# Start addresses of the on-chip tiles in a fused three-layer kernel: 32 and 64 bytes past a multiple of 128, or at the multiple

## What is computed

```python
h = rms_norm(x)              # layer 1: one projection, w_in is 2048 x 7832
nsa  = attention(h)          #   8 heads: compressed, selected and window branches, gated
rwkv = recurrence(h, h_prev) #   RWKV-7, 16 heads of 64, a 64 x 64 state each
x = x + (gated nsa, rwkv) @ w_out
x = x + mla(rms_norm(x))     # layer 2: 16 heads, latent queries and keys of 512
x = x + diff_attn(rms_norm(x))   # layer 3: 8 heads, softmax(q1 k1) - lam * softmax(q2 k2)
```

## Time and profile before

| | |
|---|---|
| median of three executions | 3158.12 us |
| the three | 3154.66, 3158.12, 3159.01 us |
| the profiled execution | span 3154.7 us, 51,865 instructions |
| TensorE busy | 3118.6 us, 99% |
| VectorE, ScalarE, GpSimd busy | 1762.0, 1274.4, 193.0 us |
| bytes read from and written to HBM | 276.05 and 44.85 MB |
| DMA queue of the loads | 34.9% of the 16 engines' span |

### The profile page before, as it was taken

One profiled execution on the slowest core, in us unless ns is written; L12 is line 12 of the kernel. 1 busy time (PEld: TensorE's weight loads), 2 busy tenths in 40 slices (PEclk: granted clock), 3 DMA queues, 4 the chain that ended last, 5 costly groups with the idle time before them and its releaser, 6 DMA issues. The chain is left out here.

```text
span 3154.7 us, 51865 instructions
## 1 busy us (share of the span) xinstructions
PE 3118.6 (99%) x21457; PEld 2553.3 (81%) x21457; DVE 1762.0 (56%) x3081; ACT 1274.4 (40%) x2328; POOL 193.0 (6%) x154
## 2 busy tenths in 40 slices
PE   8999999999999999999999999999999999999999
PEld 6877777777878778788888888888888888888787
DVE  4335565565666744644457776335556655665822
ACT  4124333433444422523346665323344434443421
POOL 0000000001011101000001010110000000000000
PEclk9999999999999999999999999999999999999999
DMA  8433333332232353343332213534223323332452
GB/s 253 114 81 91 90 94 96 100 111 60 70 98 70 110 165 108 109 110 100 107 104 54 61 51 121 163 104 117 87 81 94 94 76 99 94 95 81 158 163 77
DMA packets 494639, 324.25 MB, mean 103 GB/s; under 512 B 27194, under 2 KB 449693, under 8 KB 494406
## 3 DMA queue, kind: packets, MB, share of 16 engines
q1 hardware_dynamic: 494374, 320.94, 34.9%
q10 hardware_dynamic: 32, 0.01, 0.0%
HBM read 276.05 MB, written 44.85 MB: 102 GB/s over the span
## 5 line engine op out<-in xcount | busy, mean ns | idle before, releaser
L538 DVE TENSOR_TENSOR WLT<-AR,WHT 128x1024 fp32r<-128x1024 f32 (+1 forms) x430 | 527.0, 1231 | 668.1 <-ACT WHT L532 667.7
L550 PE MATMUL PS<-XH,WHT 128*128 128x512 f32 (+1 forms) x2224 | 896.0, 403 | 3.7 <-issue 1.4
L552 PE MATMUL PS<-XH,WLT 128*128 128x512 f32 (+1 forms) x2224 | 872.0, 392 | 0.0
L532 ACT ACTIVATE WHT<-AR 128x1024 fp32r<-128x1024 f32 (+1 forms) x430 | 447.5, 1043 | 604.9 <-PE PS L552 475.0
L551 PE MATMUL PS<-XL,WHT 128*128 128x512 f32 (+1 forms) x1712 | 668.7, 391 | 0.0
L550 PEld LDWEIGHTS PS<-XH,WHT 128*128 128x128 f32 (+1 forms) x2224 | 416.7, 187 | 101.6 <-issue 9.5
L552 PEld LDWEIGHTS PS<-XH,WLT 128*128 128x128 f32 (+1 forms) x2224 | 416.9, 187 | 97.2
L551 PE MATMUL PS<-ARR,WHT 128*128 128x512 f32 x1024 | 404.6, 395 | 0.0
L551 PEld LDWEIGHTS PS<-XL,WHT 128*128 128x128 f32 (+1 forms) x1712 | 320.9, 187 | 71.0 <-issue 4.0
L551 PEld LDWEIGHTS PS<-ARR,WHT 128*128 128x128 f32 x1024 | 192.4, 188 | 40.3 <-issue 0.2
L550 PE MATMUL PS<-XL,WHT 128*128 128x512 f32 x512 | 203.3, 397 | 0.1
(11 more groups left out here) (511 smaller groups left out, 5197.8 us busy)
## 6 DMA issues: line engine op xcount, KB each, us to landing
AR<-b_w_in SPq DMA_DIRECT2D x128, 512.0 KB, 4.0
AR<-w_in SPq DMA_DIRECT2D x122, 512.0 KB, 4.0
AR<-a_w_in SPq DMA_DIRECT2D x48, 512.0 KB, 4.5
AR<-w_out SPq DMA_DIRECT2D x32, 512.0 KB, 4.2
AR<-a_w_out SPq DMA_DIRECT2D x32, 512.0 KB, 4.0
AR<-b_w_out SPq DMA_DIRECT2D x32, 512.0 KB, 4.1
proj_scratch<-AR SPq DMA_DIRECT2D x33, 256.0 KB, 2.1
residual_scratch<-RES SPq DMA_DIRECT2D x8, 1024.0 KB, 5.4
```

What stands on the lines that cost most here:

```text
L532: self.nc.scalar.activation(self.shaped(self.high, n), self.shaped(self.raw, n), ACT.Copy).then_inc(self.s_high, 1)
L538: self.nc.vector.tensor_tensor(self.shaped(self.low, n), self.shaped(self.raw, n), f32(self.shaped(self.high, n)), ALU.subtract).then_inc( ...
L550: mm(out, wh, xh[k0 + c], start=(start and c == 0), stop=False)
L552: last = mm(out, wl, xh[k0 + c], start=False, stop=(stop and c == nk - 1))
```

## The change

Every large tile, and ARR with it, is put at a multiple of 128 bytes. A new method, fill_line, allocates an unused tile that fills up to the next such multiple; it is called ahead of RES (PAD_HEAD) and behind the constants (PAD_C). ARENA, the size of AR in words, grows from 17,064 to 17,088, a multiple of 32 words, so that what lies behind AR is at a multiple too. In the mixer of layer 1 the three input rows take 1,568 words in place of 1,539; the tiles with odd sizes (WC2, OMK) are taken last, and in nsa W2 is taken ahead of KCT.

By these sizes the addresses after are: RES, XH, XL and C as before; PAD_C 107,680 (96 bytes), PRM 107,776, STG 108,800, AR 112,896, EXT 181,248, ONESR 195,584, WHT 196,096, WLT 212,480, end 228,864. From PRM on all have remainder 0. RES before starts at 1,152, which is 9 x 128. In the mixer of layer 1, W2, TOK and BON go from remainder 12 to 0, and TW, GTI, HB, ST, LW and RQ from 76 to 0; in nsa W2 from 12 to 0. No scratch tile of layer 1 changes its region.

```diff
--- before.py
+++ after.py
@@ -57,7 +57,8 @@
 BQ0, BK0, BV0, BG0 = 0, 16, 32, 48
 LAM_INIT = 0.8 - 0.6 * float(np.exp(-0.3))
 NPROJ = 62
-ARENA = 17064
+ARENA = 17088
+LINE = 128
 SCRATCH = 1024
 EXTRA = 7
 
@@ -158,7 +159,9 @@
 
 def aligned(nc):
 
-    return (nc.sbuf_base + 31) // 32 * 32
+    base = (nc.sbuf_base + 31) // 32 * 32
+    assert base % LINE == 0, base
+    return base
 
 
 class Kernel:
@@ -167,6 +170,7 @@
     def __init__(self, nc, ctx, dram):
         self.nc, self.ctx, self.d = nc, ctx, dram
         cc, nconst = const_cols()
+        self.fill_line("PAD_HEAD")
         at = [aligned(nc)]
         self.RES = self.sb("RES", [P, KT, T])
         at.append(aligned(nc))
@@ -180,6 +184,7 @@
         self.XHT, self.XLT = ([x[:, c, :] for c in range(KT)] for x in (self.XH, self.XL))
         at.append(aligned(nc))
         self.C = self.sb("C", [P, nconst])
+        self.fill_line("PAD_C")
         self.CR = nc.alloc_sbuf_tensor_at("CR", [P, 3, T], F32R, offset=at[3] + 4 * cc["bones"][0])
         self.PRM = self.sb("PRM", [P, 2 * P])
         at.append(aligned(nc))
@@ -219,6 +224,12 @@
 
         x = self.AR[:, 24 * T:30 * T].rearrange("p (n t) -> p n t", t=T)
         return x[:, 0:TB, :], x[:, TB, :], x[:, TB + 1, :]
+
+    def fill_line(self, name):
+
+        gap = -((self.nc.sbuf_base + 31) // 32 * 32) % LINE
+        if gap:
+            self.sb(name, [P, gap // 4])
 
     def sb(self, name, shape, dt=F32):
         return self.ctx.enter_context(self.nc.sbuf_tensor(name, shape, dt))
@@ -652,8 +663,13 @@
 def first_pair_inputs(k):
 
     flat = k.RES[:, :, :].rearrange("p a t -> p (a t)")
-    n = 3 * (T + 1)
-    return flat[:, 0:n], flat[:, n:n + P], flat[:, n + P:n + P + T + 1]
+    n, m = 3 * (T + 1), lines(3 * (T + 1))
+    return flat[:, 0:n], flat[:, m:m + P], flat[:, m + P:m + P + T + 1]
+
+
+def lines(n):
+
+    return (n + LINE // 4 - 1) // (LINE // 4) * (LINE // 4)
 
 
 def nsa(k, st, tiles, ntile, res_out):
@@ -676,11 +692,12 @@
     HL, Q = KV[0][:, 0:2, :], KV[1][:, 0:2, :]
     Z, EV, S = room.tiles(2), room.tiles(2), room.tiles(3)
     PTC, TM = room.take(T), room.take(T)
-    VC, KCT = room.take(NKV * HD), room.take(NKV * NCMP)
+    VC = room.take(NKV * HD)
+    W2 = room.tiles(2, P)
+    KCT = room.take(NKV * NCMP)
     G = room.take(TB * NGATE).rearrange("p (b n) -> p b n", n=NGATE)
     MX, SIGM, HB, CST = room.take(24), room.take(NKV * NCMP), room.take(NKV * NCMP), room.take(1)
     TAB = room.take(NH)[0:NBUCKET + 1, :]
-    W2 = room.tiles(2, P)
     OH = E.rearrange("p h m -> p (h m)")[0:NBUCKET + 1, 0:T + P]
     WIN = S
     NG = NKV * NCMP
@@ -1205,12 +1222,11 @@
 
     flat, W2, WA = first_pair_inputs(k)
     take(2 * T)
-    take(3 * (T + 1))
+    take(lines(3 * (T + 1)))
     take(P)
     AR = k.STG
     TOK = chunks(5)
     BON2 = [take(T) for _ in range(2)]
-    WC2 = [take(NCH) for _ in range(2)]
     TW = take(T)
     GTI, HB, ST = (take(T).rearrange("p (c f) -> p c f", f=CH) for _ in range(3))
     IN = flat.rearrange("p (n t) -> p n t", t=T + 1)
@@ -1227,9 +1243,10 @@
     P1TA = take(2 * T).rearrange("p (c j f) -> p c j f", j=2, f=CH)
     LOT = [x.rearrange("p (c f) -> p c f", f=CH) for x in (take(T), take(T))]
     RQ = take(4 * 2 * TB).rearrange("p (n b e) -> p n b e", n=4, e=2)
-    OMK = take(NPAIR)
     QT, Y = take(T), take(T)
     EV = room.tiles(2)
+    OMK = take(NPAIR)
+    WC2 = [take(NCH) for _ in range(2)]
     FACTOR, SG = layer1_factor(k), k.EXT[:, 1, :]
     NL = len(LEVELS)
     C, B = k.c, k.PSB
```

## The result

The changed kernel takes 3164.11 us (median of seven executions, 3162.03 to 3165.41), the kernel before 3155.29 (seven, 3153.21 to 3159.01). The ratio is 1.0028, with a 95% interval of 1.0018 to 1.0037: it is slower by 0.28%, or 9 us, where 12 us less were forecast. The time lies 3 us above the upper end of the stated range (3161).

A forecast was written before the change was run, and what follows sets the result against it. TensorE, busy for 99% of the span, was taken as the bound, through the pace of its matmuls. The terms, 6.8 + 5.1 = 11.9 us less, against the median of 3158.1 gave 3146 us, with a range from 3124 to 3161.

The forecast's parts named there:

- Term 3: WHT and WLT, read by every triple, go from 64 to 0: taken as nothing, ends one step a triple either way.
- Term 1: Layer 3's 1,024 triples with ARR as moving tile: from 693.3 to 686.7 ns each, 6.8 us less.
- Term 2: Layer 3's 512 token triples with ARR as stationary tile: from 353.2 to 343.3 ns each, 5.1 us less.
- Terms 4 to 6: fp32 matmuls, DVE and ACT, and DMA into AR: each taken as nothing; fp32 and DMA with ends 1 us either way.
- The slower one: Weights and moving rows at the same place slow 1,712 triples, now at 686.7 ns, by one step: 3164 us; chance 0.10.
- The larger gain: With weights and rows both at 0, 2,736 triples drop one step, to 680 ns: 3128 us; chance 0.10.
- 0.72 for faster: The whole kernel: the chance given to its being faster by over 0.2%.

The follow-up runs named there:

- e1_weights: The kernel before with one filler of 192 bytes ahead of the weights, so only WHT and WLT move; 3164.65 us, ratio 1.0032.
- e5_rows_only: The changed kernel without its edits to nsa, rwkv and first_pair_inputs, and with a 64-byte filler ahead of the weights; 3145.46 us, ratio 0.9973.
- the first sweep: A separate kernel of matmul triples alone, 136 sets of addresses; with the weights stepped by 16 bytes, 680.0 to 702.8 ns a triple.
- e2_all_equal: The changed kernel with a 128-byte filler behind the constants, every large tile at remainder 128 modulo 256; 3133.55 us, ratio 0.9931.
- e8_all_zero: e2_all_equal with a 128-byte filler behind PAD_HEAD, so all large tiles lie at multiples of 256; 3132.82 us, ratio 0.9936.
- the second sweep: A second kernel of matmuls alone: pairs, triples, token form and fp32 by distance; pairs of 512 columns took 226.7 ns at 0, 233.3 at 128.
- e4_after_weights128: The changed kernel with a filler of 128 bytes ahead of the weights, so only WHT and WLT move; 3146.79 us, ratio 0.9973.

## Why the prediction was wrong

**What bounds the kernel: right.** The pace of the matmuls set the time and nothing else did. The difference of 8.4 us is in the distances from start to start. That the pace hangs on addresses was right as well.

**Term 3 is the step that failed.** "WHT and WLT from 64 to 0, which every triple reads: taken as nothing." It cost 10.4 ns on each triple of layers 1 and 2, more than the one step that the term gave as its end, and 17.8 us in all, more than terms 1 and 2 were to bring; e1_weights shows it alone. Its evidence was misread. The rows name the moving tile first, and by the kernel's code the moving side of L3621 to L3623 is XH and EXTR and the stationary side XL and CR, the other way round than the part on who uses which tile has it (in L3660 and L3661 likewise the stationary side is ONESR). XH, XL and CR lie a multiple of 256 bytes apart, distance 0; L3622, with XL by EXTR, is at distance 64. These rows were taken as a sample of "weights at 0"; two in three of them were a sample of "both at the same place", which the change did not bring about. The same goes for the scores, both sides in RES. The remainder was counted modulo 128, as the change itself counts, and no view was asked whether 0 and 128 modulo 256 are the same. The rows already held tiles at distance 0, 192 and 160; sorted by distance instead of by place, they would have asked for a row at distance 128 before anything was taken as nothing. Among the rows shown there was none, and the kernel before was unlikely to give one: the start addresses of its large fp32r tiles leave 128, 160 or 64 modulo 256, and no two of these differ by 128.

**Term 1: size right, reason wrong.** Forecast 6.8 us from 693.3 to 686.7 ns; measured 7.4 us, from 693.9 to 686.9. But e1_weights has the same gain with ARR left 32 bytes off (687.4), and e5_rows_only has less than half of it with ARR moved and the weights' distance to XH kept. Nor is it ARR's distance by itself: with ARR at 0 but XH and XL still at 192, the first sweep gave 700.2 ns, slower than before. The two distances act together: 192 with 160 gave 693.9, 128 with 0 gave 686.9, 128 with 96 gave 687.4. Why these pairs rank so stays open.

**Term 2: wrong.** Forecast 5.1 us less for the token form; it was 2.0 us more: 354.2 to 355.0 ns in layer 3 and, where most of the loss lies, 343.3 to 358.3 in layer 2, a part that the term did not count. In e5_rows_only, where XH stays at 192 and ARR goes to 64, it falls to 340.7. So the term's upper end was to be had, with the weights at their old distance from XH. Terms 1 and 2 without term 3 are e5_rows_only, 8 us less where 11.9 were forecast.

**Terms 4 to 6: right.** The mixer's tiles by themselves give 1.0000, L1523's counterpart takes the 276 ns of before with its stationary tile in AR, now at 0, ACT and DVE are busy as long as before, and the waits for DMA did not grow. In the groups by line and shape of the changed kernel the counterparts of the earlier trace rows read:

```profile
L1540 PE MATMUL PS<-STG,AR 64*64 64x128 f32 x256 | 15.1, 276 | 0.9 <-DVE AR L2016 0.6 <-issue 0.3
...
L1799 ACT ACTIVATE RES<-PS 128x512 f32<-128x512 f32 x32 | 19.0, 595 | 40.0 <-PE PS L1509 40.0
```

**The rivals.** The slower one named the right pair, weights and moving rows, the right triples, those of layers 1 and 2, and a time of 3164 which is the one measured. Its mechanism was the reverse of the true one. It had tiles at the same place hold each other up; e2_all_equal, with all at the same place, is with its twin e8_all_zero the fastest kernel here, and it is 128 bytes apart that costs. That the time was right is luck: it came out by cancellation. It priced one step of 6.7 ns, 11.4 us, where 17.8 were lost, kept layer 3 at its 693.3, where 7.4 us were won, and counted 5.1 us of term 2 that did not come. The larger gain named the mechanism of e2_all_equal, 680 ns with both sides alike, from the six score matmuls, and put 3128 on it; e2_all_equal took 3133.6, and the token form is more than the difference (5.1 us less counted, 4.5 more in the trace). Both were given 0.10, and against them stood rows that were of the same kind as their own. With two mechanisms of opposite sign resting on a term taken as nothing, 0.72 for faster was too much.

The rule of the Trainium skill, page "SBUF — State Buffer", section "Door 1: The DMA port swizzle" (lines of 16 bytes, a penalty where an access crosses to a new one), does not cover this: tiles at multiples of 16 bytes spread from 680 to 703 ns a triple. One detail looks like it: 16 bytes off distance 0 are free and 4, 8 and 12 are not. But no run here shows that crossing a line is the reason.

## What to carry to other kernels

Where TensorE is the bound, take the distance from start to start as the pace and sort it by the difference between the addresses of stationary and moving tiles, not by either address; multiples of 128 are no goal. Where three tiles are in play, as in a triple, take both distances together. For fp32r matmuls of 512 columns the same remainder modulo 256 for all operands gave 226.7 ns, the lowest that was measured; for 256 columns other distances do, and which ones hangs on the sequence (the token form had 113.3 ns a matmul at 112 and 192, a plain pair at 64 in one sweep and 117.8 there in the next). A kernel of matmuls alone that steps through addresses gives the table in one run, and where the kernels here had a set of the sweeps, its value held to within 5 ns a triple (the widest: distances 0 and 128, 700.0 ns in the second sweep and 695.2 in e4_after_weights128). The version with all tiles at one remainder is 0.7% faster than the kernel before and 1% faster than the changed one. A version with the token form's weights at their own distance was not tried.

## What the runs showed of the hardware

- Matmuls of 128x128 by 128x512 in fp32r take 226.7 to 236.8 ns by the placement of their operands alone, with a granted clock of 1.00 (2.4 GHz) and no other engine at work; plain fp32 ones of the same shape, which stand as two records each in the trace, start every 429.1 to 429.2 ns by record in all nine sets, distances 0 to 256 by steps of 32.
- With the rows at one place, the pace repeats every 256 bytes of distance. It is not continuous in it: 16 bytes can be worth 20 ns a triple (680.0 at 16, 700.2 at 32).
- The same set can settle on more than one pace: distance 128 gave 696.5 and 700.4 ns, and in e5_rows_only 222 of 539 triples in one stretch of layer 1's output took 700.0 and 295 took 686.7, with the addresses of the kernel before modulo 256. That is what the earlier trace rows showed already.
